# Means and spreads of the norms: one full-width product against two products of rounded parts

## The chip, the cores and the metric

The kernel runs on one core of a Trainium2 chip. The metric is the time of the whole kernel on the device in microseconds; lower is better. Engines are named TensorE (PE), VectorE (DVE), ScalarE (ACT), GpSimd (POOL) and SyncE (SP, which issues most transfers).

## The reference

Two layers on a sequence of 1024 tokens of 1024 features, all in 32-bit floats. Each layer has a mixer (a convolution branch and an attention branch side by side) and a gated MLP, each followed by a residual update with a layer norm; inside the convolution branch stands another layer norm over 512 channels.

```python
def layer_norm(x, g, b):
    mu = jnp.mean(xf, axis=-1, keepdims=True)
    var = jnp.mean(jnp.square(xf - mu), axis=-1, keepdims=True)
    y = (xf - mu) * lax.rsqrt(var + LN_EPS)
...
    h = causal_dwconv(a * jax.nn.sigmoid(g), conv_w, conv_b)
    h = jax.nn.silu(layer_norm(h, conv_ln_g, conv_ln_b))
...
    x = layer_norm(DN_ALPHA * x + (1.0 + gate) * y, ln1_g[l], ln1_b[l])
```

## The kernel before

**Layout.** Features lie on the 128 partitions and tokens along the row; the sequence is worked on in two blocks of 512 tokens (b = 0, 1). The state x has 8 tiles of 128 features.

**Slabs.** All large products are cut into 392 slabs, each 128 output features of a weight matrix (kinds g and a for the convolution branch, q, k, v, o for attention and output, ug and uv for the MLP's gate and value, d for its down-projection). A slab has 8 (for d 5 or 6) weight tiles, and each of these takes three matmuls, since weights and inputs are split in a rounded high part (type fp32r) and the rest: hi*hi (L770), hi*lo (L771), lo*hi (L772). The splitting of a slab's weights is done while the kernel runs: SyncE loads raw, ScalarE rounds it to w_hi (L957), GpSimd subtracts (w_lo, L1596). There are 4 buffers of raw and w_lo, and 3 of w_hi: ScalarE may round slab n+3 only when TensorE has finished slab n.

**Order.** Every engine runs the same loop over the slabs. In it, each first does its part of the slab (ScalarE and GpSimd also the splitting of slab n+3), and then the small steps that a table STEPS has put on that slab: taps of the convolution, attention, sums of the adaLN rows ("ad", "as"), and the norms. Each engine is strictly in order: a wait holds back all that is behind it.

**The norms.** There are 4 norms of the convolution branch (steps "cm", "cv", "cr", each with a slab of its own) and 7 of the residual stream (steps "xm", "xv", "xr"; the eighth, at the end, is done in another way and isn't touched). The texts below number them c0 to c3 and x0 to x6; they stand on slabs 20, 70, 176, 273 (cm) and 30, 102, 120, 200, 219, 298, 317 (xm). One norm goes like this:

- GpSimd adds the tiles into ssum (L1695 for c, L1707 for x).
- "m": TensorE multiplies ssum by a matrix of ones (`total`, L777), so that every partition of bank_l holds the sum for each token. VectorE centers the tiles (L1339, L1359), ScalarE squares them into tmp (L992, L1023), GpSimd adds the squares into ssum (L1678, L1685).
- "v": `totals` (L781) turns the sums so that tokens lie on partitions; VectorE works out the inverse root (`rsqrt`) and multiplies the identity with it into diag, four times 128x128 (L1319).
- "r": `spread` (L785) multiplies diag by the ones, which spreads the inverse roots over bank_l again. VectorE scales the tiles, and ScalarE and VectorE make the next inputs from them through tmp.

The sum product and the spread product are both of full 32-bit numbers. The order in which norms may use tmp is held by a list of turns (`tmp_free`).

Of the kernel before, what the change touches and what calls it, by code (L numbers as in the profile page):

```python
# [403 lines left out]
def build(nc, a):  # L404
    ctx = ExitStack()
    with ctx:
# [23 lines left out]
        ada = [sb(f"ada{i}", [P, 2, T]) for i in range(2)]  # L430
        ada_acc = [sb(f"ada_acc{i}", [P, T]) for i in range(2)]
        tmp = sb("tmp", [P, 2, T])
        ssum = sb("ssum", [P, T])
        diag = sb("diag", [P, TB, P])
        small = sb("small", [P, 2, 3, TB])
# [87 lines left out]
        first_add, ada_mul, ada_sum, ada_copied = (sem(n) for n in ("first_add", "ada_mul", "ada_sum", "ada_copied"))  # L523
        ada_add = {"pool": sem("ada_add_pool"), "dve": sem("ada_add_dve")}
        fold_step = sem("fold_step")
        y_t_done, y_evac = sem("y_t_done"), [sem("y_evac0"), sem("y_evac1")]
# [188 lines left out]
        def _(pe):  # L715
# [60 lines left out]
            def total():  # L776
                return pe.matmul(bank_l[:], ones_1, ssum[:], start=True, stop=True)  # L777

# [5 lines left out]
            def spread():  # L784
                return pe.matmul(bank_l[:], ones_1, diag[:].rearrange("p a b -> p (a b)"), start=True, stop=True)  # L785

            def x_stat(what, xi):
                if what == "xm":
                    pe.wait_ge(xsum, (DT - 1) * (xi + 1))
                    take("l", xcenter, DT * (xi + 1))  # L790
                    total().then_inc(xstat, 1)
                elif what == "xv":
                    pe.wait_ge(xsqsum, (DT - 1) * (xi + 1))
                    take("l", xsmall, SMALL * xi + 1)
                    totals().then_inc(xstat, 1)
                else:
                    pe.wait_ge(xdiag, TB * (xi + 1))
                    take("l", xscale, DT * (xi + 1))
                    spread().then_inc(xstat, 1)

            def c_stat(what, mi):
                if what == "cm":
                    pe.wait_ge(csum, (CT - 1) * (mi + 1))
                    take("l", ccenter, CT * (mi + 1))
                    total().then_inc(cstat, 1)
                elif what == "cv":
                    pe.wait_ge(csqsum, (CT - 1) * (mi + 1))
                    take("l", csmall, SMALL * mi + 1)
                    totals().then_inc(cstat, 1)
                else:  # L810
                    pe.wait_ge(cdiag, TB * (mi + 1))
                    take("l", cscale, CT * (mi + 1))
                    spread().then_inc(cstat, 1)
# [124 lines left out]
        def _(act):  # L938
# [37 lines left out]
            def second_inputs(k):  # L976
# [6 lines left out]
                act.activation(u_hi[1][:, k, :], tmp[:, k % 2, :], ACT.Copy).then_inc(ihi, 1)  # L983

            def x_square(xi, k):
                _, l, b = NORMS[xi]
                act.wait_ge(xcenter, DT * xi + k + 1)
                if k < 2:
                    act.wait_ge(*tmp_free(("x", xi)))
                else:  # L990
                    act.wait_ge(xsqsum, (DT - 1) * xi + max(k - 2, 1))
                act.activation(tmp[:, k % 2, :], xs(b, k), ACT.Square).then_inc(xsq, 1)  # L992
# [102 lines left out]
            def stage(t, src):  # L1095
# [4 lines left out]
                act.activation(stage_out[t % 4][:, 0:D // 2], src[:], ACT.Copy).then_inc(y_evac[0], 1)  # L1100

            for t in range(TB):
                evac_x(t, bank_c if t % 2 else (bank_t, bank_s))
# [11 lines left out]
            for n in range(NSLAB):  # L1115
# [45 lines left out]
                for step in STEPS[n]:  # L1161
                    what = step[0]
                    if what == "xc":
                        x_square(*step[1:])
# [48 lines left out]
        def _(dve):  # L1213
# [92 lines left out]

            def rsqrt(n, eps, which, small_done, base, diag_done):


                var, y, t = (small[:, which, i, :] for i in range(3))  # L1310

                def small_step(n, ins):
                    ins.then_inc(small_done, 1)
                    dve.wait_ge(small_done, base + n)

                small_step(1, dve.tensor_scalar(var, bank_l[:, 0:TB], 1.0 / n, eps, ALU.mult, ALU.add))
                newton(var, y, t, small_step)
                for i in range(TB):
                    dve.tensor_scalar(diag[:, i, :], ident, y[:, i:i + 1], None, ALU.mult).then_inc(diag_done, 1)  # L1319

# [21 lines left out]
            def x_rsqrt(xi):  # L1342
                dve.wait_ge(xstat, 3 * xi + 2)
                rsqrt(D, EPS / ALPHA2, 0, xsmall, SMALL * xi, xdiag)

# [16 lines left out]
            def c_rsqrt(mi):  # L1362
                dve.wait_ge(cstat, 3 * mi + 2)
                rsqrt(CONV_CH, EPS, 1, csmall, SMALL * mi, cdiag)

# [223 lines left out]
        def _(pool):  # L1589
# [65 lines left out]
            def add_ada(c, part):  # L1655
# [8 lines left out]
                else:  # L1664
                    for i in (0, 1):
                        pool.wait_ge(ada_add["pool"], n - 2 + i)
                        pool.tensor_tensor(acc[:], acc[:], rows[:, i, :], ALU.add).then_inc(ada_add["pool"], 1)  # L1667

            def second_lo(k):
                pool.wait_ge(ihi, DT + k + 1)  # L1670
# [50 lines left out]
            for n in range(NSLAB):  # L1721
# [7 lines left out]
                for step in STEPS[n]:  # L1729
                    what = step[0]  # L1730
                    if what == "hist":
                        history(*step[1:])
                    elif what == "kvh":
                        kv_history(step[1])
# [59 lines left out]
```

## Time and profile before

| what | us |
|---|---|
| median of 3 runs | 2181.25 (2179.05 to 2181.48) |
| the profiled execution | 2178.46 |
| its span, first to last instruction | 2176.7 |
| TensorE busy with matmuls | 2107.4 |
| GpSimd busy | 1399.3 |
| VectorE busy | 1187.4 |
| ScalarE busy | 1030.6 |

The mean granted clock of TensorE is 0.989 of full speed. Busy time is an average over stages: in the first 320 us TensorE waits here and there for the others, and from then on it has hardly a gap. In rows of the timeline, "x2" behind a row is the number of instructions it stands for, and the brackets give how long the engine idled before it and who ended that.

### The profile page before, as it was taken

Reading aid. Unit: us, or ns where it says so; the run is one execution under the profiler, and the core shown is the slowest. Engines: PE = TensorE matmul, PEld = TensorE weight load, DVE = VectorE, ACT = ScalarE, POOL = GpSimd, SP = SyncE. Lnnn points to the kernel's source line nnn. Section 1 sums busy time; section 2 is a strip of 40 time slices with the busy share of each in tenths; the row PEclk is TensorE's granted clock in tenths of the full one; section 3 lists DMA queues with packets and bytes.
Section 4 is the critical chain, followed back from the end, with each engine's and each line's share of the span. In section 5 each row is a group of like instructions: output and inputs, shape, how many; then the busy total and the mean of one; then the engine's idle time right before and its main releaser. Section 6 shows DMA issues by size and latency. Waiting matters only on the chain.

```text
span 2176.7 us, 27123 instructions
## 1 busy us (share of the span) xinstructions
PE 2107.4 (97%) x9515; PEld 1716.8 (79%) x9515; DVE 1187.4 (55%) x1900; ACT 1030.6 (47%) x1864; POOL 1399.3 (64%) x1767
## 2 busy tenths in 40 slices
PE   7998989999999999999999999999999999999996
PEld 6875767877888787888778888888778888888885
DVE  5797878666413554787541555587651354332224
ACT  2656346474524656354642665335462464333232
POOL 5885758675657877876546785564546776545552
PEclk9998999999999999999999999999999999999998
DMA  8633534443434344553323332332323332334332
GB/s 287 179 104 105 165 107 134 150 124 92 124 104 121 108 124 134 170 156 100 87 82 112 103 111 81 104 103 73 93 75 107 92 94 87 117 102 126 92 91 74
DMA packets 422148, 250.05 MB, mean 115 GB/s; under 512 B 49045, under 2 KB 393981, under 8 KB 422013
## 3 DMA queue, kind: packets, MB, share of 16 engines
q1 hardware_dynamic: 421146, 248.03, 38.4%
q8 instruction: 76, 1.25, 0.3%
q14 instruction: 59, 0.48, 0.1%
q10 hardware_dynamic: 867, 0.29, 0.1%
HBM read 242.71 MB, written 4.26 MB: 113 GB/s over the span
## 4 chain that ended last, share of the span: by engine, by line
PE 78%; POOL 8%; DVE 6%; issue 3%; ACT 3%; DMA 1%; SPq 1%; DVEq 0%; POOLq 0%; ACTq 0%
PE fg L770 25%; PE fg L772 24%; PE fg L771 24%; POOL w_lo L1596 4%; DVE bank_c L1291 2%; POOL ada_acc L1667 1%; PE bank_s L832 1%; POOL ssum L1678 1%; ACT ada L1087 1%; DMA first_ada<-in_w_ada_mix_dram 1%; PE bank_t L851 1%; SPq L606 1%; PE bank_l L777 0%; POOL ssum L1707 0%; PE bank_l L861 0%
## 5 line engine op out<-in xcount | busy, mean ns | idle before, releaser
L1596 POOL TENSOR_TENSOR w_lo<-raw,w_hi 128x256 fp32r<-128x256 f32 (+1 forms) x1440 | 1037.2, 751 | 690.6 <-ACT w_hi L957 689.6
L770 PE MATMUL fg<-u_hi,w_hi 128*128 128x512 f32 x2112 | 841.9, 399 | 12.6 <-DVE u_lo L1355 5.4
L772 PE MATMUL fg<-u_hi,w_lo 128*128 128x512 f32 x2112 | 825.2, 391 | 0.0
L771 PE MATMUL fg<-u_lo,w_hi 128*128 128x512 f32 x2112 | 824.9, 391 | 0.0
L957 ACT ACTIVATE w_hi<-raw 128x1024 fp32r<-128x1024 f32 (+2 forms) x392 | 379.4, 968 | 421.6 <-PE fg L772 336.4
L770 PEld LDWEIGHTS fg<-u_hi,w_hi 128*128 128x128 f32 x2112 | 398.3, 189 | 108.8 <-issue 24.3
L771 PEld LDWEIGHTS fg<-u_lo,w_hi 128*128 128x128 f32 x2112 | 398.8, 189 | 85.0 <-issue 4.8
L772 PEld LDWEIGHTS fg<-u_hi,w_lo 128*128 128x128 f32 x2112 | 398.1, 189 | 84.9
L1518 DVE SCALAR_TENSOR_TENSOR x<-fg,mod,x 128x512 f32<-128x512 f32 x160 | 119.9, 749 | 362.8 <-PE fg L772 362.8
L1291 DVE SCALAR_TENSOR_TENSOR bank_c<-glu,par,bank_c 128x512 f32<-128x512 f32 x448 | 305.3, 747 | 0.1
L770 PE MATMUL fg<-h_hi,w_hi 128*128 128x512 f32 x704 | 280.1, 398 | 0.4 <-DVE h_lo L1551 0.4
L771 PE MATMUL fg<-h_lo,w_hi 128*128 128x512 f32 x704 | 278.4, 395 | 0.0
L772 PE MATMUL fg<-h_hi,w_lo 128*128 128x512 f32 x704 | 278.4, 395 | 0.0
L1528 DVE SCALAR_TENSOR_TENSOR fg<-gate,par,fg 128x512 f32<-128x512 f32 x88 | 66.4, 755 | 358.7 <-ACT fg L1148 358.6
L770 PEld LDWEIGHTS fg<-h_hi,w_hi 128*128 128x128 f32 x704 | 132.3, 188 | 32.4 <-DVE h_lo L1551 0.9
L772 PEld LDWEIGHTS fg<-h_hi,w_lo 128*128 128x128 f32 x704 | 132.2, 188 | 32.1
L771 PEld LDWEIGHTS fg<-h_lo,w_hi 128*128 128x128 f32 x704 | 132.3, 188 | 31.4 <-issue 0.2
L1158 ACT ACTIVATE h_hi<-fg 128x512 fp32r<-128x512 f32 x88 | 52.5, 596 | 176.7 <-DVE fg L1544 176.7
L1667 POOL TENSOR_TENSOR ada_acc<-ada_acc,ada 128x512 f32<-128x512 f32 x102 | 132.3, 1297 | 4.5 <-ACT ada L1087 0.5
L1087 ACT ACTIVATE ada<-ada,ccol 128x512 f32<-128x512 f32 x136 | 90.2, 714 | 4.3 <-DMA ada<-in_w_ada_mix_dram 2.9
L1544 DVE SCALAR_TENSOR_TENSOR fg<-fg,tanh_c 128x512 f32<-128x512 f32 x88 | 61.3, 697 | 51.1 <-PE fg L772 49.9
L1153 ACT ACTIVATE tanh_c<-fg 128x512 f32<-128x512 f32 x88 | 52.7, 599 | 63.4 <-DVE fg L1531 63.4
(208 smaller groups left out, 1797.3 us busy)
## 6 DMA issues: line engine op xcount, KB each, us to landing
raw<-in_w_up_dram SPq DMA_DIRECT2D x176, 512.0 KB, 3.8
ada<-in_w_ada_ffn_dram SPq DMA_DIRECT2D x48, 512.0 KB, 4.7
raw<-in_w_down_dram SPq DMA_DIRECT2D x64, 384.0 KB, 3.4
raw<-in_w_in_dram SPq DMA_DIRECT2D x40, 512.0 KB, 3.9
raw<-in_w_down_dram SPq DMA_DIRECT2D x64, 320.0 KB, 3.1
ada<-in_w_ada_mix_dram SPq DMA_DIRECT2D x32, 512.0 KB, 4.5
first_ada<-in_w_ada_mix_dram SPq DMA_DIRECT2D x8, 1024.0 KB, 12.8
raw<-in_w_in_dram SPq DMA_DIRECT2D x32, 256.0 KB, 3.7
```

Source lines behind the costliest of these rows:

```text
L770: pe.matmul(out[:], hi[:, k, :], rhi, start=k == order[0], stop=False)
L771: pe.matmul(out[:], hi[:, k, :], rlo, start=False, stop=False)
L772: ins = pe.matmul(out[:], lo[:, k, :], rhi, start=False, stop=k == order[-1])
L957: act.activation(w_hi[n % NHI][:, 0:nk, :], raw[n % NRAW][:, 0:nk, :], ACT.Copy).then_inc(hi_ready, 1)
L1087: act.activation(ada[m % 2][:, i, :], ada[m % 2][:, i, :], ACT.Copy, scale=ccol[:, k:k + 1]).then_inc(ada_mul, 1)
L1153: act.activation(tanh_c[:], ps[:], ACT.Tanh, scale=0.5).then_inc(gate_act, 1)
L1291: ins = dve.scalar_tensor_tensor(out=conv[:, j, :] if k == CONV_K - 1 else acc[:], in0=src, scalar=w, in1=acc[:], op0=ALU.mult, op1=ALU.add)
L1518: dve.scalar_tensor_tensor(out=xs(b, k), in0=ps[:], scalar=at_gate, in1=xs(b, k), op0=ALU.mult, op1=ALU.add).then_inc(freed["dve"], 1)
L1528: dve.scalar_tensor_tensor(out=ps[:], in0=gate[:, 1:1 + T], scalar=par3[:, l, i + FT:i + FT + 1], in1=ps[:], op0=ALU.mult, op1=ALU.add).th ...
L1544: dve.scalar_tensor_tensor(out=ps[:], in0=ps[:], scalar=0.5, in1=tanh_c[:], op0=ALU.mult, op1=ALU.mult).then_inc(gate_dve, 1)
L1596: ins = pool.tensor_tensor(w_lo[n % NRAW][:, ks, :], raw[n % NRAW][:, ks, :], w_hi[n % NHI][:, ks, :].bitcast(F32), ALU.subtract)
L1667: pool.tensor_tensor(acc[:], acc[:], rows[:, i, :], ALU.add).then_inc(ada_add["pool"], 1)
```

## The change

The two products of full-width numbers become two products each, of rounded parts (fp32r). The parts lie in split, which is a second name for the memory of tmp; diag is gone, and a rounded copy of the ones, ones_r, is new. For the sum product ScalarE copies ssum into the first part, rounding it, and GpSimd subtracts that from ssum into the second. Both steps are put on the slab of "xm" or "cm", behind the splitting of weights that these engines do for the slab. For the spread product VectorE writes the four 128x128 products of the identity, rounded, into the first part, and four more instructions write what is missing into the second. At the start ScalarE copies the ones into ones_r, for which it waits for all constant loads, before it copies the first tiles of x out of the accumulators.

```diff
+        with ExitStack() as region:
+            split = sb("split", [P, 2, T], F32R, stack=region)
         tmp = sb("tmp", [P, 2, T])
         ssum = sb("ssum", [P, T])
-        diag = sb("diag", [P, TB, P])
+        ones_r = sb("ones_r", [P, P], F32R)
...
             def total():
-                return pe.matmul(bank_l[:], ones_1, ssum[:], start=True, stop=True)
+                pe.matmul(bank_l[:], ones_r[:], split[:, 0, :], start=True, stop=False)
+                return pe.matmul(bank_l[:], ones_r[:], split[:, 1, :], start=False, stop=True)
...
                 if what == "xm":
-                    pe.wait_ge(xsum, (DT - 1) * (xi + 1))
+                    pe.wait_ge(xsplit, 2 * (xi + 1))
...
+            def split_hi_of(turn, summed, count, done):
+                act.wait_ge(summed, count)
+                act.wait_ge(*tmp_free(turn))
+                act.activation(split[:, 0, :], ssum[:], ACT.Copy).then_inc(done, 1)
...
+            act.wait_ge(in_const, 16 * IN_CONST)
+            act.activation(ones_r[:], ones_1, ACT.Copy).then_inc(set_ones, 1)
             for t in range(TB):
                 evac_x(t, bank_c if t % 2 else (bank_t, bank_s))
...
                 for i in range(TB):
-                    dve.tensor_scalar(diag[:, i, :], ident, y[:, i:i + 1], None, ALU.mult).then_inc(diag_done, 1)
+                    dve.tensor_scalar(split[:, 0, i * P:(i + 1) * P], ident, y[:, i:i + 1], None, ALU.mult).then_inc(diag_done, 1)
+                for i in range(TB):
+                    dve.wait_ge(diag_done, 2 * TB * turn + i + 1)
+                    dve.scalar_tensor_tensor(out=split[:, 1, i * P:(i + 1) * P], in0=ident, scalar=y[:, i:i + 1],
+                                             in1=split[:, 0, i * P:(i + 1) * P].bitcast(F32), op0=ALU.mult, op1=ALU.subtract).then_inc(diag_done, 1)
...
+            def split_lo_of(done, n):
+                pool.wait_ge(done, n)
+                pool.tensor_tensor(split[:, 1, :], ssum[:], split[:, 0, :].bitcast(F32), ALU.subtract).then_inc(done, 1)
```

`spread` changes as `total` does, and "cm" as "xm".

On GpSimd, at slab 102 (the sum product of x1), there stands before (L1707 the last add into ssum, L1596 the low part of the weights of slab 105, L1678 the sum of squares):

```order
L1707 TENSOR_TENSOR ssum<-x,ssum 128x512 [waits x_sum,free_dve]
L1596 TENSOR_TENSOR w_lo1<-raw1,w_hi0 128x256 [waits hi_ready]
L1596 TENSOR_TENSOR w_lo1<-raw1,w_hi0 128x256 x3
L1678 TENSOR_TENSOR ssum<-tmp 128x512 [waits x_sq]
L1596 TENSOR_TENSOR w_lo2<-raw2,w_hi1 128x256 [waits hi_ready]
```

and after the change:

```order
L1732 TENSOR_TENSOR ssum<-x,ssum 128x512 [waits x_sum,free_dve]
L1617 TENSOR_TENSOR w_lo1<-raw1,w_hi0 128x256 [waits hi_ready]
L1617 TENSOR_TENSOR w_lo1<-raw1,w_hi0 128x256 x3
L1692 TENSOR_TENSOR split<-ssum,split 128x512 [waits x_split]
L1703 TENSOR_TENSOR ssum<-tmp 128x512 [waits x_sq]
L1617 TENSOR_TENSOR w_lo2<-raw2,w_hi1 128x256 [waits hi_ready]
```

The subtraction comes in between the weights of slab 105 and the sum of squares.

On ScalarE, at the same slab, before (ghist, gate, fg and tanh_c belong to the MLP's gate):

```order
L1145 ACTIVATE ghist<-fg0 128x2 [waits slab_done]
L1146 ACTIVATE gate<-fg0 128x512
L1148 ACTIVATE fg0<-fg0,par1,par3 128x512 [waits gate_act]
L957 ACTIVATE w_hi0<-raw1 128x1024 [waits slab_done,raw_in1]
L1153 ACTIVATE tanh_c<-fg0 128x512 [waits free_dve,gate_dve]
L992 ACTIVATE tmp<-x 128x512 [waits c_lo,x_center] x2
```

and after:

```order
L1158 ACTIVATE ghist<-fg0 128x2 [waits slab_done]
L1159 ACTIVATE gate<-fg0 128x512
L1161 ACTIVATE fg0<-fg0,par1,par3 128x512 [waits gate_act]
L963 ACTIVATE w_hi0<-raw1 128x1024 [waits slab_done,raw_in1]
L1166 ACTIVATE tanh_c<-fg0 128x512 [waits free_dve,gate_dve]
L994 ACTIVATE split<-ssum 128x512 [waits c_lo,x_sum]
L1003 ACTIVATE tmp<-x 128x512 [waits c_lo,x_center] x2
```

The rounding of ssum stands behind everything that ScalarE does for the slab.

On TensorE, between slab 102 (fg0) and slab 103 (fg1), before:

```order
L771 MATMUL fg0<-u_lo0,w_hi0 128x512
L772 MATMUL fg0<-u_hi0,w_lo2 128x512
L777 MATMUL bank_l<-ssum,const 128x512 [waits ada_copied,x_sum]
L770 MATMUL fg1<-u_hi0,w_hi1 128x512 [waits x_lo,free_dve,lo_ready]
L771 MATMUL fg1<-u_lo0,w_hi1 128x512
```

and after:

```order
L775 MATMUL fg0<-u_lo0,w_hi0 128x512
L776 MATMUL fg0<-u_hi0,w_lo2 128x512
L781 MATMUL bank_l<-split,ones_r 128x512 [waits ada_copied,x_split]
L782 MATMUL bank_l<-split,ones_r 128x512
L774 MATMUL fg1<-u_hi0,w_hi1 128x512 [waits x_lo,free_dve,lo_ready]
L775 MATMUL fg1<-u_lo0,w_hi1 128x512
```

The place of the product is the same; it now waits for x_split, which ScalarE and GpSimd raise, in place of x_sum.

## Rows read from the trace of the kernel before

**Rows 1.** page: busy us and share; granted clock in 40 slices; the chain's engines
```profile
PE 2107.4 (97%) x9515; PEld 1716.8 (79%) x9515; DVE 1187.4 (55%) x1900; ACT 1030.6 (47%) x1864; POOL 1399.3 (64%) x1767
...
PEclk9998999999999999999999999999999999999998
...
PE 78%; POOL 8%; DVE 6%; issue 3%; ACT 3%; DMA 1%; SPq 1%; DVEq 0%; POOLq 0%; ACTq 0%
```

**Rows 2.** page: costliest groups, busy and mean, then idle before and its releaser
```profile
L957 ACT ACTIVATE w_hi<-raw 128x1024 fp32r<-128x1024 f32 (+2 forms) x392 | 379.4, 968 | 421.6 <-PE fg L772 336.4
```

**Rows 3.** line L777: count, ns min/median/max, first and last start
```profile
L777 PE MATMUL bank_l<-ssum,const x22: 590/592/697, 191.0 to 1796.7; 128*128 128x512 f32 x22
```

**Rows 4.** timeline, TensorE alone, 716 to 722 us: start, us, engine, line, operation
```profile
719.62 1.02 PE L785 MATMUL bank_l<-diag,const 128*128 128x512 f32 x2
...
720.71 0.40 PE L771 MATMUL fg<-u_lo,w_hi 128*128 128x512 f32 x1
720.94 0.39 PE L772 MATMUL fg<-u_hi,w_lo 128*128 128x512 f32 x1
```

**Rows 5.** timeline around x1's sum product, 671 to 690 us
```profile
674.14 1.12 PE L777 MATMUL bank_l<-ssum,const 128*128 128x512 f32 x2
...
675.63 1.05 ACT L957 ACTIVATE w_hi<-raw 128x1024 fp32r<-128x1024 f32 x1
...
676.75 2.84 POOL L1596 TENSOR_TENSOR w_lo<-raw,w_hi 128x256 fp32r<-128x256 f32 x4 [2.67 <-ACT w_hi L957]
```

**Rows 6.** timeline around the sum products of c1, x2, c2, x4, c3
```profile
507.67 1.84 POOL L1596 TENSOR_TENSOR w_lo<-raw,w_hi 128x256 fp32r<-128x256 f32 x3
...
507.76 1.12 PE L777 MATMUL bank_l<-ssum,const 128*128 128x512 f32 x2 [1.46 <-POOL ssum L1695]
...
762.44 1.12 PE L777 MATMUL bank_l<-ssum,const 128*128 128x512 f32 x2 [2.01 <-POOL ssum L1707]
...
762.98 2.83 POOL L1596 TENSOR_TENSOR w_lo<-raw,w_hi 128x256 fp32r<-128x256 f32 x4 [0.60 <-ACT w_hi L957]
...
1064.83 1.13 PE L777 MATMUL bank_l<-ssum,const 128*128 128x512 f32 x2
...
1066.88 2.84 POOL L1596 TENSOR_TENSOR w_lo<-raw,w_hi 128x256 fp32r<-128x256 f32 x4 [2.21 <-ACT w_hi L957]
...
1285.55 1.02 PE L777 MATMUL bank_l<-ssum,const 128*128 128x512 f32 x2
...
1288.10 2.83 POOL L1596 TENSOR_TENSOR w_lo<-raw,w_hi 128x256 fp32r<-128x256 f32 x4 [2.48 <-ACT w_hi L957]
...
1570.14 1.13 PE L777 MATMUL bank_l<-ssum,const 128*128 128x512 f32 x2 [1.43 <-POOL ssum L1695]
...
1571.00 2.84 POOL L1596 TENSOR_TENSOR w_lo<-raw,w_hi 128x256 fp32r<-128x256 f32 x4 [0.92 <-ACT w_hi L957]
```

**Rows 7.** timeline around the sum products of c0 and x0
```profile
190.97 1.12 PE L777 MATMUL bank_l<-ssum,const 128*128 128x512 f32 x2
...
192.75 2.67 POOL L1667 TENSOR_TENSOR ada_acc<-ada_acc,ada 128x512 f32<-128x512 f32 x2
...
273.73 1.28 POOL L1678 TENSOR_TENSOR ssum<-tmp 128x512 f32<-128x512 f32 x1
```

**Rows 8.** timeline, TensorE alone, 303 to 316 us
```profile
310.70 0.76 PE L770 MATMUL fg<-u_hi,w_hi 128*128 128x512 f32 x1 [5.43 <-DVE u_lo L1355]
...
313.82 0.57 PE L771 MATMUL fg<-u_lo,w_hi 128*128 128x512 f32 x1
314.24 0.39 PE L772 MATMUL fg<-u_hi,w_lo 128*128 128x512 f32 x1
```

**Rows 9.** timeline of VectorE at x1, 705 to 722 us
```profile
716.78 0.87 DVE L1319 TENSOR_SCALAR diag<-const,small 128x128 f32<-128x128 f32 x4
```

**Rows 10.** timeline of ScalarE and GpSimd at the start, 0 to 40 us
```profile
11.15 0.60 ACT L962 ACTIVATE x<-bank_t 128x512 f32<-128x512 f32 x1
...
15.80 0.24 POOL L1612 CAST ang<-pos 128x64 f32<-128x64 int32 x1 [15.36 <-DMA rows<-in_b_ada_ffn_dram]
```

More of the change, by code:

```diff
@@ L524, in build @@
         ada_add = {"pool": sem("ada_add_pool"), "dve": sem("ada_add_dve")}
+        xsplit, csplit, set_ones = sem("x_split"), sem("c_split"), sem("set_ones")
         fold_step = sem("fold_step")
@@ L784, in spread @@
             def spread():
-                return pe.matmul(bank_l[:], ones_1, diag[:].rearrange("p a b -> p (a b)"), start=True, stop=True)
+                pe.matmul(bank_l[:], ones_r[:], split[:, 0, :], start=True, stop=False)
+                return pe.matmul(bank_l[:], ones_r[:], split[:, 1, :], start=False, stop=True)
             def x_stat(what, xi):
                 if what == "xm":
-                    pe.wait_ge(xsum, (DT - 1) * (xi + 1))
+                    pe.wait_ge(xsplit, 2 * (xi + 1))
                     take("l", xcenter, DT * (xi + 1))
@@ L796, in x_stat @@
                 else:
-                    pe.wait_ge(xdiag, TB * (xi + 1))
+                    pe.wait_ge(xdiag, 2 * TB * (xi + 1))
                     take("l", xscale, DT * (xi + 1))
@@ L802, in c_stat @@
                 if what == "cm":
-                    pe.wait_ge(csum, (CT - 1) * (mi + 1))
+                    pe.wait_ge(csplit, 2 * (mi + 1))
                     take("l", ccenter, CT * (mi + 1))
@@ L810, in c_stat @@
                 else:
-                    pe.wait_ge(cdiag, TB * (mi + 1))
+                    pe.wait_ge(cdiag, 2 * TB * (mi + 1))
                     take("l", cscale, CT * (mi + 1))
@@ L1162, in _ @@
                     what = step[0]
-                    if what == "xc":
+                    if what == "xm":
+                        split_hi_of(("x", step[1]), xsum, (DT - 1) * (step[1] + 1), xsplit)
+                    elif what == "cm":
+                        split_hi_of(("c", step[1]), csum, (CT - 1) * (step[1] + 1), csplit)
+                    elif what == "xc":
                         x_square(*step[1:])
@@ L1305, in newton, with rsqrt @@
                     small_step(3 * i + 6, dve.scalar_tensor_tensor(out=y, in0=t, scalar=1.5, in1=y, op0=ALU.add, op1=ALU.mult))
-            def rsqrt(n, eps, which, small_done, base, diag_done):
+            def rsqrt(n, eps, which, small_done, base, diag_done, turn):
                 var, y, t = (small[:, which, i, :] for i in range(3))
@@ L1343, in x_rsqrt @@
                 dve.wait_ge(xstat, 3 * xi + 2)
-                rsqrt(D, EPS / ALPHA2, 0, xsmall, SMALL * xi, xdiag)
+                rsqrt(D, EPS / ALPHA2, 0, xsmall, SMALL * xi, xdiag, xi)
             def x_scale(xi, k):
@@ L1363, in c_rsqrt @@
                 dve.wait_ge(cstat, 3 * mi + 2)
-                rsqrt(CONV_CH, EPS, 1, csmall, SMALL * mi, cdiag)
+                rsqrt(CONV_CH, EPS, 1, csmall, SMALL * mi, cdiag, mi)
             def c_scale(mi, k):
@@ L1732, in _ @@
                         history(*step[1:])
+                    elif what == "xm":
+                        split_lo_of(xsplit, 2 * step[1] + 1)
+                    elif what == "cm":
+                        split_lo_of(csplit, 2 * step[1] + 1)
                     elif what == "kvh":
```

## The prediction

> **What bounds the kernel now.** First the page: TensorE is busy for 97% of the span and holds 78% of the chain that ended last, while GpSimd is busy for 64% [rows 1]. So from the first mixer on, time that TensorE loses is time of the kernel, and time that it saves is a gain; the other engines count where TensorE waits for them. Then the two lines that the change rewrites: the sum product L777 has 22 records of 0.59 us, two for each of 11 norms, and the spread product L785 as many [rows 3]. I call the norms c0 to c3 (convolution) and x0 to x6 (residual). Then the timeline around each L777, with one question: what have ScalarE and GpSimd still to do, in their order, when TensorE arrives there? Last the group of L957, ScalarE's rounding of weights: it idles 421.6 us, and 336.4 of that end with a matmul of TensorE [rows 2]. That is the three buffers of w_hi: slab n+3 is rounded only when slab n is multiplied.
>
> **The product itself.** Where nothing is waited for, L785 starts at 719.62 and the second matmul of the next slab at 720.71; the matmuls of the slabs follow each other every 0.23 us [rows 4]. So the full-width product takes 720.71 - 719.62 - 0.23 = 0.86 us of TensorE. The two new products have the type and size of the slabs' own matmuls, 2 x 0.23 = 0.46, in the same accumulation. That saves 0.40 us a time. There are 22 products; two at x0 lie behind other waits, so 20 x 0.40 = 8.0 us go. The bounds are 0 (two records before, two after) and 22 x (1.18 - 0.46) = 16; I take the value by start times, because ends are modelled.
> On this, the Trainium skill's page "FP8 and Floating Point Precision", section "TensorE Precision Notes", says that true FP32 takes four passes through the array. The records show two instructions, but the time between starts, 0.86 us or nearly four times 0.23, agrees with four. By two passes the saving would be nothing, by four it is the one I use.
>
> **The parts in front of the sum product.** Before, TensorE could multiply ssum as soon as the last GpSimd add was done, which mostly happened during the slab. Now ScalarE must round ssum and GpSimd must subtract. In the code both steps stand in the slab of "xm" or "cm", behind the weight work of slab n+3; and that weight work can only begin when TensorE is done with slab n, the very point at which it now stops and waits. So nothing hides the parts. At x1, TensorE starts L777 at 674.14; ScalarE begins w_hi at 675.63, GpSimd's w_lo runs from 676.75 for 2.84 us [rows 5]. The subtraction of 128x512 comes behind that; GpSimd's nearest row, an add of the same size, takes 1.28 us [rows 7]. TensorE can go on at 676.75 + 2.84 + 1.28 = 680.87, 6.7 us later. ScalarE's own part ends in that time. The same sum for the others, w_lo's end + 1.28 - the old start of L777 [rows 6]:
> x3 and x5 repeat x1 (6.7 each); x4 1288.10 + 2.83 + 1.28 - 1285.55 = 6.7, and x6 repeats it; x2 762.98 + 2.83 + 1.28 - 762.44 = 4.7; c1, where the slab is a short one, 507.67 + 1.84 + 1.28 - 507.76 = 3.0; c2 1066.88 + 2.84 + 1.28 - 1064.83 = 6.2; c3 1571.00 + 2.84 + 1.28 - 1570.14 = 5.0. Together 5 x 6.7 + 4.7 + 3.0 + 6.2 + 5.0 = 52.4 us. TensorE is the bound there, so I count them in full.
> At c0 two adds of adaLN rows stand in front as well: 192.75 + 2.67 + 1.28 - 190.97 = 5.7 us [rows 7]. At x0 what comes next waits for GpSimd's sum of squares rather than for TensorE. It began at 273.73 [rows 7]; now it has to wait for the subtraction (275.0), the product, two centerings and a square, about 2.6 us by their rows' sizes of 0.5 to 0.7, so it starts near 277.6: 3.9 us. With these, waits come to 62.0 us.
>
> **The parts in front of the spread product.** VectorE gets four more instructions of 128x128. The nearest row is the four that are there, 0.87 us together [rows 9]; I take 0.9, at most double with two inputs from memory. At x1 they ended at 717.65 while TensorE came at 719.62, so they are hidden, and the other norms but c0 and x0 have two slabs between sum of squares and spread as well. Only c0 pays in the open: +0.9, and a wait of about as much behind its sum product fills up, so I add nothing. If that cover were gone, 11 x 0.9 = 10 us would be the most.
>
> **The clock.** Eleven new waits of 3 to 7 us make TensorE idle as it hardly is now. The one gap of this length, 5.43 us before 310.70, was followed by matmuls every 0.42 us, until 314.24 [rows 8]: 3.5 us of work at the lower of the two levels, 1.2 GHz, of which 1 - 0.23/0.42 = 45% is lost, 1.6 us. I charge that at each of the nine late norms and at c0: 16 us. Bounds: nothing (behind the gaps of 1.4 and 2.0 us at the old c3 and x2 [rows 6] the page's row of the clock stays at 9 [rows 1]), and twice that, 32, if half speed lasts twice as long.
>
> **The start.** ScalarE's first copy ran at 11.15; now a copy of the ones stands in front, which needs all the small constant loads, and GpSimd waited for the same until 15.80. That is 4.7 us later [rows 10]. What of it reaches the first slab lies between 0 and 4.7; TensorE waits for loads of x and of the adaLN rows in this time anyway, so I take a value near the lower end, 1.
>
> **Sum.** 62 - 8 + 16 + 1 = +71 us. The profiled execution took 2178.46 us (span 2176.7), so 2249.5; the median of the runs shown, 2181.25, lies 2.8 above it, so I forecast 2252.
>
> **Rivals.**
> 1. *The waits come, the clock stays up.* For it: gaps of 2 us did no harm. Against: the 5.43 us gap did. 62 - 8 + 1 = +55: 2236.
> 2. *Half of the waits is made up.* While TensorE stands, the others run ahead, and waits that come later would shrink. Against: after 320 us it hardly waits at all, the page has 97% busy, so there is nothing to shrink. 31 us less, with less clock cost: +35, 2216.
> 3. *The clock costs double*, or the parts of the spread come late too: +16 to +20: 2270.
> 4. *Faster.* If ssum's parts were ready when TensorE arrives, only the products would count: -8 + 1, 2174. It decides on whether GpSimd's subtraction gets in before the w_lo of slab n+3. It would need w_hi to be rounded before slab n ends; the 336 us that ScalarE waits for TensorE and the order of the code speak against it.
> 5. *It doesn't do what it says:* the new products still run at full-width cost. Then +8 on top, 2260, inside the range.
>
> **How the numbers follow.** Forecast 0.55 (its own range 2240 to 2262), rival 1 0.15, rival 2 0.10, rival 3 0.12, rival 4 0.03, rival 5 0.05. The range reaches over rivals 1, 3 and 5 and the edge of 2: 2220 to 2276. A measurement of this kernel tells 0.2%, some 4 us, from no change. Faster has rival 4 alone, 0.03; the same 0.02; slower 0.95.
>
> **What would show it.** In the profile after: the line of the sum product waits for GpSimd's split, eleven times, 3 to 7 us each, some 60 us in all, and the wait ends right behind a w_lo group; each product takes 0.46 us between starts; the granted clock shows a stretch at half level behind most of the waits; the spread product waits little. The forecast is wrong if TensorE finds the split done, if the wait is much shorter since GpSimd takes the subtraction first, or if the clock stays at full level through gaps of 6 us.

## The result

The changed kernel takes 2262.1 us (median of 4 runs, 2261.48 to 2262.69) against 2180.97 us for the kernel before (4 runs, 2179.05 to 2181.48). The ratio is 1.0377, 95% interval 1.0361 to 1.0392: 81 us slower. The forecast was 2252, range 2220 to 2276, so the time lies in the range, 10 us above the forecast. The profiled execution of the changed kernel has a span of 2259.9 us at a granted clock of 0.966, where the one before had 2176.7 us and 0.989.

The page of the kernel after; these lines answer to [rows 1] and [rows 2]:

```profile
span 2259.9 us, 27201 instructions
...
PE 2122.6 (94%) x9515; PEld 1732.9 (77%) x9515; DVE 1198.4 (53%) x1944; ACT 1037.0 (46%) x1876; POOL 1413.1 (63%) x1778
...
PEclk7997989999999999999999999999999999999998
...
PE 72%; POOL 12%; issue 6%; DVE 4%; ACT 4%; SPq 1%; DMA 1%; DVEq 0%; POOLq 0%; ACTq 0%
...
L963 ACT ACTIVATE w_hi<-raw 128x1024 fp32r<-128x1024 f32 (+2 forms) x392 | 379.3, 968 | 423.3 <-PE fg L776 353.2
```

TensorE has as many instructions as before (9515), yet it is busy for 15 us more, and its share of the chain fell from 78% to 72% while GpSimd's rose from 8% to 12%. The busy time of the other engines grew by 6 to 14 us and doesn't explain 81. The row of the clock reads 9 in all slices but four (all but two before), three of them among the first six; a digit there hides stretches of a few microseconds.

The waits of TensorE in the kernel after, the largest first (engine, tile, line, releaser: total us, times, longest):

```profile
PE bank_l L781 <- POOL split L1692: 67.7, 11, 6.6
PE bank_t L731 <- ACT x L968: 6.8, 1, 6.8
PE bank_l L790 <- DVE split L1339: 6.1, 2, 3.1
...
PE fg L774 <- DVE u_lo L1376: 4.7, 1, 4.7
```

The first line holds most of the result: 11 waits, one for each norm, in front of the first matmul of the sum product, for GpSimd's subtraction. Before, TensorE stood at this place four times, 5.7 us in all, for GpSimd's last add:

```profile
PE bank_l L777 <- POOL ssum L1695: 2.9, 2, 1.5
PE bank_l L777 <- POOL ssum L1707: 2.8, 2, 2.0
```

In the list after, the third line is the spread product's, 2 times only. The fourth is the wait of [rows 8], a little shorter.

The timeline of the kernel after around x1's sum product, which answers to [rows 5] (start, us, engine, line, operation, and in brackets the idle time before it and who ended that):

```profile
695.06 1.29 POOL L1732 TENSOR_TENSOR ssum<-x,ssum 128x512 f32<-128x512 f32 x1
...
696.10 0.39 PE L776 MATMUL fg<-u_hi,w_lo 128*128 128x512 f32 x1
...
697.89 1.04 ACT L963 ACTIVATE w_hi<-raw 128x1024 fp32r<-128x1024 f32 x1
...
699.02 2.77 POOL L1617 TENSOR_TENSOR w_lo<-raw,w_hi 128x256 fp32r<-128x256 f32 x4 [2.67 <-ACT w_hi L963]
...
700.08 0.62 ACT L994 ACTIVATE split<-ssum 128x512 fp32r<-128x512 f32 x1
701.74 1.26 POOL L1692 TENSOR_TENSOR split<-ssum,split 128x512 fp32r<-128x512 f32 x1
...
703.06 0.79 PE L781 MATMUL bank_l<-split,ones_r 128*128 128x512 f32 x1 [6.58 <-POOL split L1692]
...
703.65 0.63 PE L782 MATMUL bank_l<-split,ones_r 128*128 128x512 f32 x1
...
704.08 0.63 PE L774 MATMUL fg<-u_hi,w_hi 128*128 128x512 f32 x1
...
704.50 0.63 PE L775 MATMUL fg<-u_lo,w_hi 128*128 128x512 f32 x1
```

Read it from the top. ssum is whole at 696.35, about when TensorE ends its slab. From there the sum product could run, but ScalarE is still to round the weights of the slab three ahead (to 698.93), and GpSimd to subtract for them (to 701.79); the subtraction for the norm, 1.26 us, comes last. TensorE idles 6.58 us, and the matmuls behind that start 0.42 to 0.43 us apart where they stood 0.23 apart in [rows 4]. The windows around it say the same of the clock (stretch, its length, busy us and count of each engine, granted clock, DMA share, GB/s):

```profile
690.00:696.00 6.00, 6.00 (x28) 4.99 (x27) 0.75 (x1) 1.06 (x1) 4.63 (x6) 1.00 0.30 87
696.00:703.00 7.00, 0.48 (x3) 0.06 (x1) 1.51 (x2) 3.50 (x6) 4.33 (x6) 0.89 0.26 75
703.00:708.30 5.30, 5.24 (x12) 4.13 (x13) 1.89 (x3) 1.26 (x2) 1.27 (x2) 0.50 0.00 2
708.30:714.00 5.70, 5.70 (x26) 4.69 (x25) 2.21 (x4) 1.55 (x3) 0.00 (x0) 1.00 0.17 50
```

Full level (2.4 GHz) before, 12 matmuls in 5.3 us at the lower level (1.2 GHz) behind the wait, 26 in 5.7 us after that.

**Where the 83 us of span went.** I compared the start of each slab on TensorE in the two traces; what that difference grows by at a slab is its step. (Behind a product the record of a slab's first matmul overlaps the product's, so there the start is taken as the second matmul's, less the distance from the second to the third.) At the nine late norms (c1 to c3, x1 to x6) there are two steps, one at the wait and one in the slab behind it:

| norm | wait forecast | step at the wait | step in the slab behind |
|---|---|---|---|
| c1 | 3.0 | 3.05 | 2.33 |
| x1 | 6.7 | 6.72 | 1.95 |
| x2 | 4.7 | 4.65 | 2.25 |
| c2 | 6.2 | 6.60 | 1.09 |
| x3 | 6.7 | 6.74 | 1.04 |
| x4 | 6.7 | 6.75 | 0.88 |
| c3 | 5.0 | 4.98 | 0.86 |
| x5 | 6.7 | 6.71 | 1.12 |
| x6 | 6.7 | 6.75 | 1.60 |
| sum | 52.4 | 52.9 | 13.1 |

Behind these slabs the nine late spread products save about 0.4 us each, 3.7 in all; 2.0 are lost behind x2's, 1.4 behind those of x1, x3 and c3, and 0.2 at slab 156. Together that is the 66 us by which the difference grows from slab 38 to the end. The other 17.3 us are there at slab 38, of which the last experiment puts 5 down to the execution.

### The profile page after: what moved, and what is told of

It reads as the page before. It is cut to its first block, busy times and chain, and to the rows that moved or that the text cites. A ratio compares the mean times of both kernels' runs of the same rounds, so it can differ in the third digit from the quotient of the medians.

```text
span 2259.9 us, 27201 instructions
## 1 busy us (share of the span) xinstructions
PE 2122.6 (94%) x9515; PEld 1732.9 (77%) x9515; DVE 1198.4 (53%) x1944; ACT 1037.0 (46%) x1876; POOL 1413.1 (63%) x1778
## 4 chain that ended last, share of the span: by engine, by line
PE 72%; POOL 12%; issue 6%; DVE 4%; ACT 4%; SPq 1%; DMA 1%; DVEq 0%; POOLq 0%; ACTq 0%
PE fg L774 23%; PE fg L776 23%; PE fg L775 23%; POOL w_lo L1617 6%; POOL ada_acc L1688 3%; POOL ssum L1703 1%; PE bank_s L838 1%; DVE bank_c L1308 1%; ACT w_hi L963 1%; POOL split L1692 1%; ACT ada L1098 1%; DMA first_ada<-in_w_ada_mix_dram 1%; SPq L610 0%; PE bank_t L857 0%; DVE fg L1549 0%
## 5 line engine op out<-in xcount | busy, mean ns | idle before, releaser
L774 PEld LDWEIGHTS fg<-u_hi,w_hi 128*128 128x128 f32 x2112 | 404.0, 191 | 106.8 <-issue 19.2
L776 PEld LDWEIGHTS fg<-u_hi,w_lo 128*128 128x128 f32 x2112 | 403.0, 191 | 87.0
L775 PEld LDWEIGHTS fg<-u_lo,w_hi 128*128 128x128 f32 x2112 | 403.8, 191 | 82.7
```

The costliest lines, as they stand in the source:

```text
L774: pe.matmul(out[:], hi[:, k, :], rhi, start=k == order[0], stop=False)
L775: pe.matmul(out[:], hi[:, k, :], rlo, start=False, stop=False)
L776: ins = pe.matmul(out[:], lo[:, k, :], rhi, start=False, stop=k == order[-1])
```

## The experiments

In all of them what is computed stays the same; the two that fill the wait do matmuls on top, whose result is thrown away.

**The two halves of the change.** The first kernel keeps the parts of the sum product and gives the spread product back its one matmul of full width; VectorE's four extra instructions go too.

```diff
             def spread():
-                pe.matmul(bank_l[:], ones_r[:], split[:, 0, :], start=True, stop=False)
-                return pe.matmul(bank_l[:], ones_r[:], split[:, 1, :], start=False, stop=True)
+                return pe.matmul(bank_l[:], ones_1, tmp[:, 0, :], start=True, stop=True)
```

> Only the sum product is split; the spread product is of full width again, from one row of tmp. My theory: the whole loss is in the waits of the sum product, so this keeps them (some 68 us of TensorE waiting at its line) and gives back what the spread product saved (9 x 0.4 us) and what VectorE's extra work cost at c0 and x0 (about 2 us): 2263 us, within 3 us of the change. The rival, that splitting the spread product has a good share in the loss: 2250 or less.

The second does the reverse: ssum is multiplied in full width as before, and only the spread is made of parts.

```diff
             def total():
-                pe.matmul(bank_l[:], ones_r[:], split[:, 0, :], start=True, stop=False)
-                return pe.matmul(bank_l[:], ones_r[:], split[:, 1, :], start=False, stop=True)
+                return pe.matmul(bank_l[:], ones_1, ssum[:], start=True, stop=True)
```

> Only the spread product is split; ssum goes into the sum product at full width as before. My theory: no wait of length, so it is the kernel before with 9 x 0.4 us saved, about 2 us lost at c0 and x0 and 1 us at the start: 2179 to 2181 us. Rival as in the run with the sum product only: 2190 or more.

Measured: sum only 2258.35 us, ratio 1.0351 (1.0336 to 1.0367); spread only 2184.69, ratio 1.0012 (1.0003 to 1.0022), against 2183.21 for the kernel before in the same job. Together 1.0363, about the 1.0377 of the whole change. The first lies 4.7 us under the 2263 expected, outside its 3 us, but far from the rival's 2250; the second lies 3.7 over the 2181 expected, for a reason shown below. The first has the eleven waits to the last digit:

```profile
PE bank_l L781 <- POOL split L1687: 67.7, 11, 6.6
```

So the loss is the sum product's. But the second is no gain either, although its nine late spread products are 0.38 to 0.42 us shorter each. At three of them something is given back behind: 0.5 us at x1, 0.6 at x3, 0.3 at c3. The most is lost at x2. These are rows of its timeline there:

```profile
809.96 0.87 DVE L1331 TENSOR_SCALAR split<-const,small 128x128 fp32r<-128x128 f32 x4
...
810.75 1.13 DVE L1334 SCALAR_TENSOR_TENSOR split<-const,small,split 128x128 fp32r<-128x128 f32 x4
...
811.80 0.68 DVE L1553 SCALAR_TENSOR_TENSOR tanh_c<-tanh_c,fg 128x512 f32<-128x512 f32 x1
...
813.32 0.60 ACT L1170 ACTIVATE h_hi<-fg 128x512 fp32r<-128x512 f32 x1 [7.27 <-DVE fg L1560]
...
813.82 1.05 ACT L962 ACTIVATE w_hi<-raw 128x1024 fp32r<-128x1024 f32 x1
...
814.94 2.84 POOL L1612 TENSOR_TENSOR w_lo<-raw,w_hi 128x256 fp32r<-128x256 f32 x4 [5.82 <-ACT w_hi L962]
...
820.44 1.48 PE L866 MATMUL bank_t<-const,ada_acc 128*128 128x1 f32 x8 [1.61 <-POOL ada_acc L1683]
```

The four new VectorE instructions (1.13 us) stand in front of the gate of the slab; ScalarE waits for that gate (7.27 us, 6.21 in the kernel before), and behind h_hi stand w_hi, GpSimd's w_lo and the adaLN sums, for which TensorE now waits 1.61 us (0.13 before), also with slower matmuls behind it. Between the starts of slabs 129 and 134 this kernel falls 3.2 us behind the kernel before: steps of 1.5 and 2.8 us, of which 0.7 and 0.4 come back at slabs 133 and 134. That is with the product's own saving of 0.4 in it, so the spread of x2 in parts costs 3.6 us there. In the whole change it is the same chain with steps of 1.1 and 1.6 us, 1.6 net and 2.0 without the saving.

At x1 and x3 the chain is the same and the wait small: the adaLN sum behind the next slab waits 0.27 and 0.32 us for GpSimd in this kernel, and not at all in the kernel before. At x1:

```profile
730.52 1.05 PE L866 MATMUL bank_t<-const,ada_acc 128*128 128x1 f32 x8 [0.27 <-POOL ada_acc L1683]
```

At c3 it is a wait of 0.18 us for ScalarE's probs_t, which I didn't follow further.

**Wait or clock?** The third keeps the wait and takes away the idleness: TensorE multiplies into bank_l, where the sum product writes over it, while it would wait.

```diff
+            def fill(count):
+                for _ in range(count):
+                    pe.matmul(bank_l[:], ones_r[:], u_hi[SLABS[now[0]][2]][:, 0, :], start=True, stop=True)
...
-                    pe.wait_ge(xsplit, 2 * (xi + 1))
                     take("l", xcenter, DT * (xi + 1))
+                    fill(20)
+                    pe.wait_ge(xsplit, 2 * (xi + 1))
```

> The change, but TensorE multiplies 12 to 20 matmuls whose result is thrown away into bank_l while it waits for the parts of ssum (4.5 us of the 6.5). The end of the wait doesn't move. Theory that the clock takes part of the loss: it stays at full level, each norm gains 1 to 2 us and the product 0.4, so 2262 - 16 = 2246 us. Rival, that the clock costs nothing and the extra is something else (banks, later waits): 2262.

Measured: 2249.48 us, ratio 1.0307 (1.0291 to 1.0322) against 2183.21, clock 0.978. That is 13 us under the changed kernel (15 by the ratios) with GpSimd's subtraction as late as it was. Yet the filling ended too early, and 11 waits remain, 21.1 us in all. Around x1:

```profile
689.64 3.33 PE L797 MATMUL bank_l<-u_hi,ones_r 128*128 128x512 f32 x14
695.05 0.50 PE L781 MATMUL bank_l<-split,ones_r 128*128 128x512 f32 x1 [2.08 <-POOL split L1701]
695.40 0.40 PE L782 MATMUL bank_l<-split,ones_r 128*128 128x512 f32 x1
695.64 0.40 PE L774 MATMUL fg<-u_hi,w_hi 128*128 128x512 f32 x1
...
696.56 0.61 PE L775 MATMUL fg<-u_lo,w_hi 128*128 128x512 f32 x1
696.98 0.63 PE L776 MATMUL fg<-u_hi,w_lo 128*128 128x512 f32 x1
```

Here the matmuls run at full level for 1.5 us behind the wait, and only then at the lower one, for 3.4 us. With 28 matmuls at the x norms (25 at x0) and 19 to 27 at the c norms, in the place of 20 and of 12 to 18, the wait is filled to its end:

> As the run with fillers before, but 19 to 28 thrown-away matmuls, so that the whole wait is filled. In that run 2 us of idling were left and the clock still fell for 3.4 us at seven of the norms, at 1.4 us each. Theory: now it doesn't fall at the late norms, and 9 x 1.4 = 13 us more come back: 2237 us. Rival, that the 1.4 us are not the clock's: 2249.

Measured: 2242.11 us, ratio 1.0289 (1.0274 to 1.0304) against 2178.98, clock 0.988, the lower level for 58 us in all (49 before, 158 after, of which 24 lie between 25.7 and 49.5 us, where no time is lost: slab 0 starts at 45.03 in both the trace before and the one after). Around x1:

```profile
696.79 0.50 PE L781 MATMUL bank_l<-split,ones_r 128*128 128x512 f32 x1 [0.32 <-POOL split L1701]
697.13 0.40 PE L782 MATMUL bank_l<-split,ones_r 128*128 128x512 f32 x1
697.36 0.40 PE L774 MATMUL fg<-u_hi,w_hi 128*128 128x512 f32 x1
```

Now the product runs at full level: from its start to the slab's first matmul 0.57 us (0.34, with its weight load in the open behind a wait, and 0.23), where the kernel after has 704.08 - 703.06 = 1.02. The steps in the slab behind the wait are gone at all nine late norms (under 0.1 us), and the steps at the waits are 0.3 to 0.4 us smaller at each. From slab 38 on this kernel gains 16.5 us on the changed one: 13.2 for the slabs behind the waits, and the other 3.3 are about 9 x 0.4 for the sum products themselves. So the waits alone cost nearly 3%, and the lower clock, on the slabs and on the products, 20 us of the 81 (19 by the ratios).

**A longer wait.** GpSimd does its subtraction twice, which makes each wait some 1.3 us longer.

```diff
+                pool.tensor_tensor(split[:, 1, :], ssum[:], split[:, 0, :].bitcast(F32), ALU.subtract).then_inc(dose, 1)
+                pool.wait_ge(dose, doses[0])
                 pool.tensor_tensor(split[:, 1, :], ssum[:], split[:, 0, :].bitcast(F32), ALU.subtract).then_inc(done, 1)
```

> The change with GpSimd's subtraction of ssum done twice, one behind the other: 1.3 us more in front of each sum product. Theory that TensorE is the bound and GpSimd's subtraction the last thing that it waits for: 11 x 1.3 = 14 us more, 2276. Rival, that something else ends the waits: 2262.

Measured: 2273.06 us, ratio 1.0433 (1.0417 to 1.0448), 11.0 us over the changed kernel.

```profile
PE bank_l L782 <- POOL split L1698: 82.2, 11, 7.9
```

The waits grew by 14.5 us, 1.3 each, so GpSimd's last instruction is what TensorE waits for, one for one: at the nine late norms the steps grow by 12.0, at c0 and x0 by 2.4. Of this 11.2 reach the end of the span, since the steps behind the waits are smaller: by 2.3 us at c0 and x0, where TensorE waits for other things as well, by 0.4 in the slabs behind the nine, and by 0.6 behind x2. The stretches at the lower level, which begin within the wait, add up to 162 us (158 after): 1.3 us more of wait don't make the loss by the clock larger.

**Order against time.** Two ways to take the wait away. In one, both parts stay on their slab, but in front of its weight work on ScalarE and GpSimd (c0 excepted):

```diff
+                for step in STEPS[n]:
+                    if step[0] == "xm":
+                        split_lo_of(xsplit, 2 * step[1] + 1)
+                    elif step[0] == "cm" and step[1]:
+                        split_lo_of(csplit, 2 * step[1] + 1)
                 if n + NHI < NSLAB:
                     split_lo(n + NHI)
```

> The change with both parts of ssum ahead of the weight work of the slab, on ScalarE and GpSimd, at all norms but c0; the product stays where it is. Theory: what is left is ScalarE's 0.6 and GpSimd's 1.3 us behind the last sum, so a wait of about 2 us at ten norms, no fall of the clock, and the products' saving: 2181 + 17 + 9 x (2 - 0.8) = 2209 us. Rival, that the weight work now comes too late and TensorE waits for w_lo instead: a wait at L774 shows, and the time stays above 2230.

Measured: 2213.81 us, ratio 1.0159 (1.0142 to 1.0176): 48 of the 81 us are gone by order alone. What is left at x1:

```profile
690.44 1.29 POOL L1735 TENSOR_TENSOR ssum<-x,ssum 128x512 f32<-128x512 f32 x1
...
691.76 0.63 ACT L994 ACTIVATE split<-ssum 128x512 fp32r<-128x512 f32 x1 [4.18 <-POOL ssum L1735]
...
692.47 1.26 POOL L1695 TENSOR_TENSOR split<-ssum,split 128x512 fp32r<-128x512 f32 x1 [0.74 <-ACT split L994]
...
693.78 0.50 PE L781 MATMUL bank_l<-split,ones_r 128*128 128x512 f32 x1 [1.92 <-POOL split L1695]
```

That is the bare chain, rounding 0.63 and subtraction 1.26 behind the last add, and it is the least that this change can cost as long as the product stands where ssum has only just become whole. The steps at the late waits are 1.1 to 2.1 us in the place of 3.0 to 6.8. That is 4.8 us over the 2209 expected: the clock was to stay up, and behind four of the nine late waits (c1, x2, c2, x5) it still fell, for 6.8 us in the steps of the slabs behind.

In the other, the parts stay where the change put them, and the product and the centering move one slab on (c0 and x0 excepted):

```diff
+        put(m, "xs", xi)
+        m += xi > 0
         put(m, "xm", xi)
```

> The parts stay on their slabs; the sum product and the centering come one slab later at all norms but c0 and x0 (4 us of matmuls stand between then). Theory: the parts are 6.7 us behind TensorE at most, of which 5.5 are hidden by the slab, so the waits of nine norms fall to 1 us or so, the clock stays up, and the products' saving of 0.4 us each comes out: 2181 + 17 (c0, x0 and the start) + 9 x (1.2 - 0.8) = 2202 us. Rival: the later centering makes the sums of squares late, and the wait turns up at the next product: 2220 or more.

Measured: 2199.53 us, ratio 1.0083 (1.0066 to 1.01). Around x1:

```profile
693.81 1.27 POOL L1697 TENSOR_TENSOR split<-ssum,split 128x512 fp32r<-128x512 f32 x1
...
695.13 0.50 PE L786 MATMUL bank_l<-split,ones_r 128*128 128x512 f32 x1 [1.20 <-POOL split L1697]
```

The expectation reckons with 4 us of matmuls between the two; a slab has 5.5, and still 1.20 us of wait are left, as the 6.6 us of wait less a slab of matmuls would have it. From slab 34 on this kernel loses only 4.7 us to the kernel before; the rest lies ahead of that, mostly at c0 and x0, which were left alone.

**The start.** The copy of the ones is moved behind the first splitting of weights.

```diff
-            act.wait_ge(in_const, 16 * IN_CONST)
-            act.activation(ones_r[:], ones_1, ACT.Copy).then_inc(set_ones, 1)
             for t in range(TB):
                 evac_x(t, bank_c if t % 2 else (bank_t, bank_s))
...
             split_hi(2)
+            act.wait_ge(in_const, 16 * IN_CONST)
+            act.activation(ones_r[:], ones_1, ACT.Copy).then_inc(set_ones, 1)
```

> The change with the copy of the ones moved behind the first copies of x and of the parameters. Theory: at the start the change loses 0.8 us by the shift of the second slab pair, so 2261 us, and TensorE's 6.8 us of waiting for ScalarE at its third tile of x is gone. If the whole start is hidden otherwise: 2262 and no difference.

Measured: 2262.06 us against 2262.1 with the copy in front. TensorE's wait of 6.8 us for ScalarE's copy of x, second in the list of waits above, is gone, and nothing is won: it now waits 4.6 us for transfers of x. So the start costs nothing that can be measured; by slab 20 the trace after is also level, within 0.1 us, with that of the last kernel below, which has no copy of the ones.

**Everything hidden.** Both remedies together, the ones late, and in full width what has no cover: both products of c0, the sum and the spread of x0, the spread of x2.

```diff
-                    pe.wait_ge(xsplit, 2 * (xi + 1))
+                    pe.wait_ge(*((xsplit, 2 * xi) if xi else (xsum, DT - 1)))
                     take("l", xcenter, DT * (xi + 1))
-                    total().then_inc(xstat, 1)
+                    total(xi == 0).then_inc(xstat, 1)
...
-                    spread().then_inc(xstat, 1)
+                    spread(xi in (0, 2)).then_inc(xstat, 1)
```

> Parts of ssum ahead of the weight work, sum product and centering one slab later, copy of the ones late; c0 and x0 keep both full-width products, x2 keeps the full-width spread. Theory: nothing waits for the parts any more and the reduced products give 0.4 us each, 9 for sums and 8 for spreads: 2181 - 7 = 2174 us, faster than the kernel before. Rival, that the parts cost as much elsewhere (GpSimd's queue, a later sum of squares): 2181 or more.

Measured: 2176.67 us (11 runs), ratio 0.9973 (0.9964 to 0.9982) against 2181.04: faster than the kernel before, by 0.3%. Around x1:

```profile
678.39 1.29 POOL L1746 TENSOR_TENSOR ssum<-x,ssum 128x512 f32<-128x512 f32 x1
...
679.71 0.63 ACT L1004 ACTIVATE split<-ssum 128x512 fp32r<-128x512 f32 x1 [4.18 <-POOL ssum L1746]
...
680.41 1.29 POOL L1706 TENSOR_TENSOR split<-ssum,split 128x512 fp32r<-128x512 f32 x1 [0.74 <-ACT split L1004]
...
682.73 2.83 POOL L1631 TENSOR_TENSOR w_lo<-raw,w_hi 128x256 fp32r<-128x256 f32 x4 [1.03 <-ACT w_hi L973]
...
685.09 0.39 PE L789 MATMUL bank_l<-split,ones_r 128*128 128x512 f32 x1
```

The subtraction ends at 681.70, 3.4 us ahead of the product, and the product has no idle time in front. Does the gain come from the new products, or from their place? One more kernel is the kernel before with its sum product a slab later, in full width.

```diff
+        m += xi > 0
         put(m, "xm", xi)
...
         m, v, r, o = ns
+        m += 1
         put(m, "cm", mi)
```

> The kernel before, with both products of full-width numbers, and the sum product (with the centering behind it) one slab later at all norms but c0 and x0; nothing else changes. It tells where the gain of the version with everything hidden (2176.67 against 2181.04) comes from. Theory A, the place: before, TensorE idled 1.46, 2.01 and 1.43 us in front of the sum products of c1, x2 and c3, for GpSimd's last add; one slab later these 4.9 us are gone, so this kernel gains about 4.9 us of 2181 or 0.22%, 2176, as much as the hidden version, and the products of parts bring nothing on top. Theory B, the products: the 18 shorter products of the hidden version (0.40 us each, 7 us) bring the gain, and what the place gives is lost again by the centering and the squares, which then run later: this kernel shows 2181 within 0.1%.

Measured: 2177.81 us (11 runs), ratio 0.9986 (0.9976 to 0.9995) against 2180.13. Both theories hold in part. The place gives about half: the gaps of 1.46 and 2.01 us in front of c1 and x2, and 1.43 at c3 [rows 6], are gone, and with the product's new place reckoned in, 1.8, 2.3 and 1.7 us are won there; some comes back where what follows the norm is now later, 1.5 us at slab 74 and 1.1 at slab 130. From slab 34 on this kernel gains 3.5 us on the kernel before, the hidden one 6.7. The two intervals overlap by a little, so the 3.2 us for the products of parts are what single traces show and not more than likely. Set against each other, the two traces also show where parts still cost something: the hidden kernel loses 1.0 us each at x1 and x3, where its adaLN sum waits, and nothing at x2, whose spread it does in full width. That bears out the cause given above for x2's loss. Whether full width at x1 and x3 too would win those 2 us wasn't tried.

This kernel shows a second thing. Up to slab 34 its instructions are those of the kernel before, and yet its trace is 5.2 us behind the trace of before there (2.7 at slab 20). The kernel before itself took 2177.37 to 2184.57 us in the 15 runs of this job. So about 5 of the 17.3 us that the trace of the changed kernel has lost by slab 38 are what one execution differs from another by, and not the change. This rests on one trace of each kernel.

## Why the prediction was right, and where it was off

**What bounds the kernel.** Right. A wait of TensorE is time of the kernel: the steps of the slabs follow the waits, and doubling the subtraction made each wait 1.3 us longer.

**The product itself.** The size was right, the place wrong. By start times the full-width sum product took 0.96 us at x1 in the kernel before (674.14 to the slab's second matmul at 675.33, less 0.23), and the two of parts take 0.57 in the filled kernel, so 0.39 less; a spread product in parts saves 0.38 to 0.42 us. Rival 5 (full cost) is out. The Trainium skill's page "FP8 and Floating Point Precision", section "TensorE Precision Notes", gives true FP32 four passes through the array; the traces agree, with 0.86 to 0.96 us for a product whose parts take 0.23 us each back to back. But of the sum products none was saved: all of them stand directly behind the wait, where the clock is down, so they take 1.02 us there, no less than the one of full width at full level. The prediction charged the low clock to the slab behind and booked the saving at full level: 9 x 0.40 = 3.6 us too favourable. The nine late spread products did save 3.7 us, as forecast.

**The parts in front of the sum product.** Right, and the heart of it: 52.4 us forecast for the late norms, 52.9 measured, eight of nine within 0.05 us. The ninth, c2, is 0.4 over, and why stays open. At c0 and x0 the trace after must be set against one with the same start. Against the kernel with the later full-width product, c0 costs 6.8 us and x0 5.4; forecast were 5.7 + 1.6 for the clock less 0.4 for the product, 6.9, and 3.9. x0 was 1.5 too low; nothing was charged there for the clock behind the wait, which would be about as much.

**The parts in front of the spread product.** Put at nothing, and wrong at x2, in small at x1, x3 and c3. I called them hidden since two slabs lie between, and looked only at whether TensorE would find diag in time, which it did. Who else waits for VectorE was not asked: at x2 the slab's gate does, and through ScalarE and GpSimd the adaLN sums. 2.0 us in the whole change, 3.6 with the spread alone. At x1 and x3 the same chain takes 0.5 and 0.6 us, more than the product saves, and at c3 0.3 are lost. At c0, where I expected nothing net, the slab behind the spread starts 0.9 us later than in the trace before, and just so in the kernel with the later full-width product, so the parts cost nothing there.

**The clock.** Right in kind and in size: 14.4 us for the nine, 13.1 measured. Single steps lie between 0.9 and 2.3 where 1.6 was charged to each, so the sum is better than its parts, and that is luck. The lower level also took the saving of the sum products, as said above. Rival 1 (the clock stays up) and rival 3 (double) are out by that.

**The start.** +1 was forecast and nothing found, inside its bounds of 0 to 4.7.

**The sum.** For the late part the forecast has 52.4 + 14.4 - 7.2 = 59.6, and the traces 65.9: 0.5 more wait, 1.3 less clock, 3.6 for the sum products, 2.0 at x2's spread, 1.4 at the spreads of x1, x3 and c3, and some tenths. For the early part it has 11.4, and the traces 17.3 - 5.2 = 12.1. So 7 of the 10 us are terms that were mis-sized. The other 3 are no term of the change: the 5.2 us by which the trace after is the later of two executions, less the 2.8 that the forecast added to get from one execution to the median, and 0.4 more between span and time.

**The other rivals.** Of the late waits nothing was made up later, as rival 2 had it; only behind x0, in the stretch where TensorE waits for others anyway, 2.8 us were. Rival 4, the parts ready in time, needed another order of the code, as the prediction said; with it, a later product and full width in five places it came true at 2176.67, where the rival had 2174.

## What to carry to other kernels

On a strictly ordered engine, a small step that others wait for belongs in front of the bulk work of its slab, and its consumer a slab behind it. Ask of each added instruction not only whether its own consumer is late but who else is queued behind it on its engine. A faster matmul directly behind a new wait can save nothing: here, behind waits of 4.5 to 6.6 us, it ran at the lower level, so price both at that level.

## What the runs showed of the hardware

- **How long a gap is doesn't say by itself what the clock does.** In the kernel before, 2.01 us of idle in front of x2's sum product [rows 6] left the granted clock at full level on both sides. In the first filled kernel, 2.08 us at x1 were followed by 3.4 us at the lower level, which began 1.5 us after work had gone on:

```profile
758.00:762.40 4.40, 2.43 (x11) 1.69 (x9) 0.43 (x1) 1.90 (x4) 4.38 (x6) 1.00 0.19 54
762.40:766.00 3.60, 3.56 (x14) 2.61 (x15) 2.97 (x5) 2.22 (x4) 2.83 (x4) 1.00 0.31 91
```

```profile
693.00:696.56 3.56, 1.50 (x6) 1.24 (x7) 0.72 (x2) 0.00 (x0) 2.00 (x3) 1.00 0.02 5
696.56:699.96 3.40, 3.40 (x9) 2.63 (x8) 1.16 (x2) 1.26 (x2) 1.27 (x1) 0.50 0.01 2
```

The first fence is the kernel before around x2, the second the first filled kernel around x1, in the columns of the windows above; the last three numbers of a row are clock, DMA share and GB/s. The version with the parts first shows it within one kernel: at x1, x3 and x5 TensorE idles 1.92 us in front of the product, and behind x1 and x3 the level stays, while behind x5 it falls 1.5 us after work has gone on, for 3.4 us. What sets the one from the other stays open.

- **After waits of 4.5 to 6.6 us the lower level was there from the first matmul on** at all eleven norms, since it began within the wait: for x1, the windows of the result show 0.89 as the mean over the wait and 0.50 from its end, until 708.3.
- **VectorE's scalar_tensor_tensor of 128x128** takes 1.13 us for four in a row, against 0.87 for four tensor_scalar of the same size: 0.26 us more for the form that reads a second tensor.
